# The order in which the two heads of a pair issue their half-width matmuls, in two blocks of attention and retention

## The reference, cut to what matters

```python
# block 1, windowed attention: 8 heads of 64, query block b sees key blocks b-1, b, b+1
p = softmax(q k^T * scale, with a sink logit per head)
o = einsum('bnkgqj,bnjkd->bnqkgd', p, vb)            # values

# block 1, retention in both directions: 8 heads of 64, chunks of 128 tokens
inner = (q k^T) * dmat;   out_inner = inner v
cross = (q * xi) states                              # once per direction
ret = out_inner + cross(forward) + cross(backward)

# block 2, dilated causal attention: 3 groups of 4 heads of 64
e = exp(s - mx); den = sum(e)
o = (e v) / den;  lse = mx + log(den)                # merged over the groups by mx and den
```

## Time and profile before

| | |
|---|---|
| median of 3 runs | 2928.59 us |
| the profiled execution, its own time | 2928.59 us |
| its span | 2926.8 us |
| TensorE busy | 2803.0 us, 96% |
| TensorE weight load busy | 2242.2 us, 77% |
| VectorE, ScalarE, GpSimd busy | 55%, 32%, 46% |
| mean granted TensorE clock | 0.986 |
| DMA, mean over the span | 52 GB/s |

### The profile page before, as it was taken

One profiled execution on the slowest core, in us unless ns is written; L12 is line 12 of the kernel. 1 busy time (PEld: TensorE's weight loads), 2 busy tenths in 40 slices (PEclk: granted clock), 3 DMA queues, 4 the chain that ended last, 5 costly groups with the idle time before them and its releaser, 6 DMA issues. The chain is left out here.

```text
span 2926.8 us, 36614 instructions
## 1 busy us (share of the span) xinstructions
PE 2803.0 (96%) x13748; PEld 2242.2 (77%) x13748; DVE 1600.3 (55%) x2419; ACT 925.8 (32%) x1793; POOL 1333.6 (46%) x1012
## 2 busy tenths in 40 slices
PE   6999989999999999999999899999899999999997
PEld 4777778778888888777766688878777788888886
DVE  7866665574555555542367741143378655555555
ACT  5655422232222222333344410121243322222222
POOL 2332332456665556543222234445614665566553
PEclk9999999999999999999999999999999999999998
DMA  3101002111111111131101011131101111111111
GB/s 121 37 30 37 31 19 80 46 45 54 51 58 51 48 54 49 46 116 37 37 30 38 30 38 56 50 115 65 65 25 34 58 59 44 51 51 51 61 47 65
DMA packets 71375, 151.94 MB, mean 52 GB/s; under 512 B 6448, under 2 KB 29360, under 8 KB 70064
## 3 DMA queue, kind: packets, MB, share of 16 engines
q1 hardware_dynamic: 64256, 123.76, 13.0%
q10 hardware_dynamic: 6960, 26.01, 2.3%
HBM read 141.36 MB, written 8.39 MB: 51 GB/s over the span
## 5 line engine op out<-in xcount | busy, mean ns | idle before, releaser
L601 POOL TENSOR_TENSOR WH<-WRAW,CST 128x512 fp32r<-128x512 f32 x204 | 227.7, 1116 | 898.8 <-PE PS L717 756.2
L715 PE MATMUL PS<-XH,WH 128*128 128x512 f32 x1248 | 514.5, 412 | 2.8 <-DVE XL L1992 2.7
L717 PE MATMUL PS<-XH,WL 128*128 128x512 f32 x1248 | 489.1, 392 | 0.0
L716 PE MATMUL PS<-XL,WH 128*128 128x512 f32 x1248 | 488.5, 391 | 0.0
L626 POOL TENSOR_TENSOR WL<-WRAW,WH 128x512 fp32r<-128x512 f32 x216 | 310.1, 1436 | 285.0 <-ACT WH L1620 284.1
L2375 DVE TENSOR_TENSOR H<-H,PS 128x512 f32<-128x512 f32 x352 | 235.5, 683 | 174.6 <-PE PS L1012 174.4
L715 PEld LDWEIGHTS PS<-XH,WH 128*128 128x128 f32 x1248 | 235.5, 189 | 85.2 <-issue 38.5
L1620 ACT ACTIVATE WH<-WRAW 128x512 fp32r<-128x512 f32 x204 | 129.0, 633 | 487.4 <-PE PS L1012 398.9
L1010 PE MATMUL PS<-HH,WH 128*128 128x512 f32 x704 | 277.5, 394 | 5.3 <-DVE HL L2309 5.3
L1012 PE MATMUL PS<-HH,WL 128*128 128x512 f32 x704 | 281.1, 399 | 0.0
L603 POOL TENSOR_TENSOR WL<-WRAW,WH 128x512 fp32r<-128x512 f32 x204 | 271.7, 1332 | 16.0
(11 more groups left out here) (323 smaller groups left out, 5042.2 us busy)
## 6 DMA issues: line engine op xcount, KB each, us to landing
WRAW<-ws SPq DMA_DIRECT2D x104, 512.0 KB, 3.4
WRAW<-ws SPq DMA_DIRECT2D x176, 256.0 KB, 2.6
RAWX<-ws SPq DMA_DIRECT2D x88, 256.0 KB, 2.7
H<-xT ACTq DMA_DIRECT2D x4, 1024.0 KB, 11.2
H<-xT ACTq DMA_DIRECT2D x2, 2048.0 KB, 10.3
h_spill<-H ACTq DMA_DIRECT2D x1, 4096.0 KB, 11.8
H<-h_spill ACTq DMA_DIRECT2D x4, 1024.0 KB, 8.0
outT<-H ACTq DMA_DIRECT2D x4, 1024.0 KB, 4.4
```

The source lines that it names most:

```text
L601: pool.tensor_tensor(WH[:, j, c], WRAW[:, j, c], ONES[:, 0:1].to_broadcast((P, 512)), ALU.mult).then_inc(hi_split, 1)
L715: pe.matmul(out, WH[:, j, w], rh(kt), start=(n == 0), stop=False)
L716: pe.matmul(out, WH[:, j, w], rl(kt), start=False, stop=False)
L717: last = pe.matmul(out, WL[:, j, w], rh(kt), start=False, stop=(n == len(kts) - 1))
```

## The change

Three loops are turned round. In `values1` and `values2` the loop over heads goes outside, so that one head's matmuls all come before the other's; in `values2` the two spreading matmuls of a head now follow its values. In `r_outs` three loops over the eight (pair, head) blocks, one for each kind of product, become one loop, which does all products of a block before the next block. The start flag is set accordingly. Numbers and operands of the matmuls are the same; so are all waits and semaphores, and their places at the head and end of each function.

```diff
 values1:
-                for kt in range(nk):
-                    for hh in range(2):
+                for hh in range(2):
+                    for kt in range(nk):
                         last = pe.matmul(PS[64 * hh:64 * hh + 64, OB, 0:P], V1[...], PT1[:, kt, blk(hh)], ...)
 r_outs:
-                pairs = [(j, hh, slice(64 * hh, 64 * hh + 64)) for j in range(4) for hh in range(2)]
-                if c > 0:
-                    for j, hh, r in pairs:
-                        pe.matmul(PS[r, OB + hh, blk(j)], FST[r, c % 2, j], QX[r, c % 2, 0, j], start=(j == 0), stop=False)
-                if c < NB - 1:
-                    for j, hh, r in pairs:
-                        pe.matmul(PS[r, OB + hh, blk(j)], BST[r, c, j], QX[r, c % 2, 1, j], start=(c == 0 and j == 0), stop=False)
-                for j, hh, r in pairs:
-                    last = pe.matmul(PS[r, OB + hh, blk(j)], RV[...], SI[:, c % 2, hh, j], start=False, stop=(j == 3))
+                for j in range(4):
+                    for hh in range(2):
+                        r = slice(64 * hh, 64 * hh + 64)
+                        out = PS[r, OB + hh, blk(j)]
+                        first = True
+                        if c > 0:
+                            pe.matmul(out, FST[r, c % 2, j], QX[r, c % 2, 0, j], start=True, stop=False)
+                            first = False
+                        if c < NB - 1:
+                            pe.matmul(out, BST[r, c, j], QX[r, c % 2, 1, j], start=first, stop=False)
+                        last = pe.matmul(out, RV[...], SI[:, c % 2, hh, j], start=False, stop=True)
 values2:
-                for kt in range(nk):
-                    for hh in range(2):
-                        r = slice(64 * hh, 64 * hh + 64)
+                for hh in range(2):
+                    r = slice(64 * hh, 64 * hh + 64)
+                    for kt in range(nk):
                         pe.matmul(PS[r, OB, 0:P], V[...], PT2[:, s % 2, kt, blk(hh)], ...)
-                for n, c in ((1, 6), (2, 0)):
-                    for hh in range(2):
-                        r = slice(64 * hh, 64 * hh + 64)
+                    for n, c in ((1, 6), (2, 0)):
                         last = pe.matmul(PS[r, OB, blk(n)], stat2(s, c + hh).to_broadcast((P, 64)), IDENT,
                                          start=True, stop=True)
```

More of the change, by code:

```diff
@@ L922, in r_outs @@
                     pe.wait_ge(r_copied, c)
-                pairs = [(j, hh, slice(64 * hh, 64 * hh + 64)) for j in range(4) for hh in range(2)]
-                if c > 0:
-                    for j, hh, r in pairs:
-                        pe.matmul(PS[r, OB + hh, blk(j)], FST[r, c % 2, j], QX[r, c % 2, 0, j], start=(j == 0), stop=False)
-                if c < NB - 1:
-                    for j, hh, r in pairs:
-                        pe.matmul(PS[r, OB + hh, blk(j)], BST[r, c, j], QX[r, c % 2, 1, j], start=(c == 0 and j == 0), stop=False)
-                for j, hh, r in pairs:
-                    last = pe.matmul(PS[r, OB + hh, blk(j)], RV[:, c, j * P + 64 * hh:j * P + 64 * hh + 64],
-                                     SI[:, c % 2, hh, j], start=False, stop=(j == 3))
+                for j in range(4):
[8 more added lines that the diff above has]
+                            pe.matmul(out, BST[r, c, j], QX[r, c % 2, 1, j], start=first, stop=False)
+                        last = pe.matmul(out, RV[:, c, j * P + 64 * hh:j * P + 64 * hh + 64], SI[:, c % 2, hh, j],
+                                         start=False, stop=True)
                 last.then_inc(r_out, 1)
```

## The result

| | before | after |
|---|---|---|
| median of 4 runs | 2928.41 us | 2993.55 us (2992.10 to 2995.47) |
| ratio | | 1.0221, 95% interval 1.0209 to 1.0233 |
| the profiled execution, own time and span | 2928.59, 2926.8 | 2993.47, 2991.7 |
| mean granted clock | 0.986 | 0.984 |

The account below looks back on a forecast made before the run. TensorE, busy 96% of the span, was taken as the bound. The terms 12.1 (values1) + 25.5 (values2) + 36 (r_outs) - 2 (waits) gave 71.6, say 72, on 2928.6: 3001 us, range 2956 to 3030.

Parts of the forecast that it names:

- The bound: In both attentions and the retention's second part, TensorE is the bound, so its added time lengthens the whole run.
- The waits of the earlier trace: TensorE's waits for VectorE in block 2 and the retention, 16.7 us, were to take in 2 us.
- The slot: Time of two passes side by side on different column halves, 0.108 us; a lone pass was priced the same.
- Rival 4: In all three functions, a lone 64-column pass takes half a slot, 0.054 us; 2926 us in all, chance 0.04.
- r_outs: In the retention, lost partners and added changes of shape cost 4.8 us in chunks 1 to 6, 4.0 in 0 and 7.
- Rival 3: In the retention, sparser passes let the clock fall to 1.2 GHz, adding 19 to 38 us; chance 0.17.
- A change of shape: In r_outs, every change of weight shape was taken to cost the block allowance, about 0.16 us, whatever cells come next.
- The bound of 12.7 us for r_outs: Lower bound in r_outs if shapes on different cells run side by side without emptying the array.
- The values: In values1 and values2, lost partners add 12.1 and 25.5 us, together 37.6.
- I take one matmul, the only depth that the trace shows: In values1 and values2, TensorE looks one matmul ahead, so a step of P passes takes P - 2 slots.
- the rival of far lookahead: In values1 and values2, TensorE looks past all head 0's matmuls, costing nothing; 2964 or 2941 us in all, chance 0.25.
- Strict order: In values1 and values2, at most one pass overlaps between heads, adding 46.2 us; 3009 to 3018 us in all, chance 0.12.

Follow-up runs that it names:

- e4: Kernel before, but in r_outs each head's quarter-size matmuls come together, then each head's half-size ones, with no change of shape added; 2942.3 us, ratio 1.0043.
- e5: Kernel before, but in r_outs each pair does FST, BST and RV before the next pair, heads alternating, so shapes change more often; 2937.67 us, ratio 1.0026.
- e1: Kernel before with only r_outs in the changed order, values1 and values2 as before; 2970.9 us, ratio 1.0138.
- e7: Kernel before, but each values2 step moved to stand directly ahead of the next scores2, saving one change of shape per step; 2949.59 us, ratio 1.0072.
- e8: Kernel before, but the next step's scores2 stands directly behind values2, which stays in place, from each head group's third step on; 2944.59 us, ratio 1.0052.
- e3: Kernel before, but in values1 and values2 the heads alternate after every two matmuls, r_outs as before; 2933.9 us, ratio 1.0017.

## Why the prediction was right

- **The bound.** TensorE was the bound in all three places: 64.9 us more span, 64.3 us more busy time. The waits of the earlier trace rows got shorter by 2.4 us, put at 2.
- **The slot.** A pass of 128 columns on 64 columns of weights, alone, takes as long as a pair: 0.109 us in e4 and in the changed kernel. Rival 4, a lone pass at half the price, fell.
- **r_outs.** Put at 36 us. By chunk the change measured 4 x 4.60 + 2 x 4.34 + 3.45 + 7.3 = 37.8. Of that 7.3 - (5.8 - 2.05) = 3.5 us are chunk 0 at the lower clock. The others came out slightly below the forecast: a block took 0.94 us and not 0.97, and the last three chunks are followed by spreading matmuls of the same shape, so that one change of shape less stands at their end. Rival 3 (the clock falls) happened, in one chunk of eight.
- **A change of shape costs the same** whatever cells come next: 0.36 us for two RV passes ahead of the other head's FST, and 0.15 us each with both heads in flight (e5). The bound of 12.7 us for r_outs fell. The runs show the price; that TensorE is emptied is inferred from it. The Trainium skill says that a change of tiling mode drains TensorE ("TensorEngine Tiling (Array Packing)", Tiling Modes), and these figures agree.
- **The values: the mis-sized term.** The step was "I take one matmul, the only depth that the trace shows". The trace showed only that at least one is passed over. Measured, a matmul on the free half passes over three waiting passes. That makes steps of 12 passes 0.26 us longer instead of 0.43, of 16 passes 0.49 instead of 0.65, and those of 8 the same instead of 0.22 longer: 24 x 0.26 + 26 x 0.26 + 22 x 0.49 = 24 us instead of 37.6. It lies between the forecast and the rival of far lookahead. Strict order, which would have cost 46, fell; the sentence of the Trainium skill that matmuls start in program order ("TensorE: Matmul & The Clock Gate", Part 3) does not hold between two column halves here, as the rows at 1513.46 show.
- **The sum.** Values 13.6 us below and the retention 5 above its 36. Of the 41.0 us there, 37.8 are `r_outs`; the rest goes with the lower clock around it, on both sides of chunk 0 (0.6 and 0.8 us) and between chunks 4 and 5 (1.6 us). Behind the last `values2` 2.5 us more were measured. There the clock was low for 40.0 us, 25.2 of them busy, against 36.6 and 20.8 before, an estimated 2 us; e1, whose block 2 is as before, has 2.1 more there too, so it does not come from the values.
- **Luck.** That 65.1 us came so near to 72 is in part luck: the values were put at half as much again as they cost, and the lower clock, which stood in the forecast only as a rival, gave back some 6 us of the miss around the retention. With the right depth and the rest of the working as it was, the forecast would have been 24 + 36 - 2 = 58 us, as far below the result as 72 lay above it.

## What to carry to other kernels

Two matmuls that each use one half of the array run side by side only if the second stands near enough in the queue: here with at most three waiting passes of the other half between them, and of the orders tried only alternating the halves cost nothing in every step. Group such matmuls by the shape of their weights first and alternate halves within a group; each change of shape costs about as much as one and a half full passes of 128 columns. Read overlap from the time between starts, or from the busy union against the sum of durations: the mean of one pass shows next to nothing of it. And count the lower clock before an order is called no better: by the estimates above, e7 and e8 saved their changes of shape and lost more by new waits and a lower clock.

## What the runs showed of the hardware that was not expected

- TensorE starts a float32 pass on a free column half (or quarter) while three passes of the other half stand ahead of it in program order, not two and not four: 8, 12, 16 and 32 passes in a block, of shapes 128*64 and 64*64, all fit one depth. Whether it counts passes or instructions, and per half or in all, is open.
- Where a second block of four passes stands at that depth, the other half's weights are not loaded ahead, which costs 0.05 us (e3); a second block of two costs nothing there.
- A drop of the granted clock that begins around a wait lasts longer with sparse passes behind it: 3.4 us in six kernels with the old chunk 0, 6.8 to 17.1 in four with a sparser one, while equally sparse passes that begin at the upper level kept it (chunks 1 to 3).
